# A 27-stage transformer kernel: an opening in another order, a mean summed on VectorE, two norms apart, two norms by token columns, and products of ones

## The chip, the core and the metric

The kernel runs on one NeuronCore of a Trainium2 chip. The metric is the device time of one execution in microseconds (us); less is better. Three runs of the kernel before gave 1297.25, 1302.40 and 1303.61 us, median 1302.4.

## The reference

Two blocks run over one sequence of 256 tokens with width D = 1024, all in float32. Only the parts that the change touches are shown in detail.

```python
def first_block(x, mem, ...):
    for i in range(2):
        if i == 0:
            h = rms_norm(x, norm_mix[0])
            u = h @ w_pw1 + b_pw1; a, gate = split(u, 2)            # 1024 -> 2048
            u = causal depthwise conv, 31 taps, of a * sigmoid(gate)
            x = x + silu(layer_norm(u)) @ w_pw2 + b_pw2
        else:
            x = x + diff_attention(rms_norm(x, norm_mix[1]), k, v of rms_norm(x, kv_norm), ...)
        x = x + memory_cross_attention(rms_norm(x, norm_mem[i]), mem, ...)   # 256 memory tokens
        x = x + swiglu(rms_norm(x, norm_ffn[i]), ...)                        # hidden 2816
    return rms_norm(x, norm_final)

def second_block(x, ...):
    h = x                                              # what norm_final gave
    w = rms_norm(h, attn_pre_norm) @ w_in              # then three-branch and sliding-window attention
    mixed = concat(rms_norm(o_nsa), rms_norm(o_swa)) @ w_out
    h = h + rms_norm(mixed, attn_post_norm)
    u = causal_dwconv(rms_norm(h, ffn_pre_norm) @ w_up, conv_w, conv_b)   # 3 taps, width 5632
    gate, up = split(u, 2)
    y = (gelu(gate) * up) @ w_down
    return h + rms_norm(y, ffn_post_norm)
```

## The kernel before

Activations lie turned: 128 partitions hold features, the 256 tokens run along the free dimension, and a matrix of 1024 features is 8 chunks, handled in 4 pairs of 512 columns. Weights come in tiles of 1 MB (1024 rows by 256 columns), in the order of `PLAN`. To keep float32 accuracy each tile and each activation is split: ScalarE copies it to a rounded high part (`whi`, two halves, L865 and L868), VectorE subtracts to the low part (`wlo`, L1224 and L1231), and TensorE makes three products for each pair of blocks (L470 to L472), 48 matmuls of 256 columns for a tile. Memory keys and values (`memk`, `memv`) are multiplied whole in float32 (L504).

**Order.** The order on every engine is written out by hand; semaphores tie them. There are two buffers (`raw`, `whi`, `wlo`, `acc`, each 0 and 1). The helper `ahead` stands for tile t + 2: ScalarE's copy may begin when TensorE is done with tile t, VectorE's subtraction follows it in VectorE's own order, and SP issues the next load (L389, L394) once VectorE is done with the raw data. Each engine works strictly in its order.

**Norms.** ScalarE squares (L917, L1066, L1147, L1192), GpSimd adds the four pairs into one where the name is in `SUMMED` (L435), TensorE multiplies with a matrix of ones, which sums over the features into `st` (L605), and VectorE takes the inverse root over 128x256 in 12 operations (L1269 to L1281). RMS norms scale results, not inputs: the matrix product does not wait for the norm, only its evacuation (`times_r`) does. For the output norms of the last attention the squares are summed into columns instead, one token to a partition (L630); the root is then taken of 128x4 values (`norm_columns`), and `spread` (L639) multiplies the column, broadcast, with the identity so that each partition holds the row of tokens.

**Opening.** SP loads the gains, x, tiles 0 and 1, constants, positions and memory (L376 to L385), then tile 2 on. VectorE: norm `mix0`, the subtraction for tile 2, and then per tile evacuations, subtractions, gates (`gated`) and portions of the 31-tap convolution (19 taps on VectorE, 12 as products on ScalarE added by GpSimd). TensorE goes from `pw1` (8 tiles) into `memk` (4) and `memv` (8). The mean of the layer norm is 8 products with ones (L763) set among the value tiles, the last of them behind the fifth. VectorE then centres (L1672), makes rotation angles (L1678 to L1692), subtracts for `pw2` tile 0, takes the norm, and scales (L1696).

**`win`.** Its inputs are normed twice, by `norm_final` and by `attn_pre_norm`; `Hhi` carries both gains and two square sums are made, of SQ and of SQF. GpSimd adds both in turns, and TensorE multiplies both with ones behind tile 0, ahead of tile 1.

**The end.** After the last attention: `spread("out2")`, four pairs scaled and split, `wout` (4 tiles), norm `post2`, X += normed, pairs split again, `up2` (22 tiles in 11 turns, with a 3-tap convolution on VectorE and ScalarE), `down2` (12 tiles), norm `fpost2`, X += normed, and four stores of pairs.

## Time and profile before

| what | before |
|---|---|
| median of 3 runs | 1302.4 us |
| the profiled execution | 1303.29 us |
| its span, first to last instruction | 1301.5 us |
| TensorE busy | 1197.5 us, 92% |
| VectorE busy | 909.4 us, 70% |
| ScalarE busy | 604.8 us, 46% |
| GpSimd busy | 107.9 us, 8% |
| mean granted TensorE clock | 0.958 |
| weights and inputs read | 193.08 MB |

Line numbers (L470) are those of the kernel before. PE is TensorE, PEld its weight loads, DVE VectorE, ACT ScalarE, POOL GpSimd, SP SyncE. An instruction of the timeline is: start, duration, engine, line, operation, output<-input, shape, count, and in brackets the idle time before it and what ended that. Times are us from the start of the span. A float32 matmul shows as two records, so `x4` on L605 is two products.

### The profile page before, as it was taken

The page shows a single profiled execution, that of the slowest core. Times are in us where ns is not written, and L with a number is a line of the kernel's source. Part 1 is how long each engine was busy: PE and PEld are TensorE (multiplying, and loading weights), DVE is VectorE, ACT ScalarE, POOL GpSimd, SP SyncE. Part 2 cuts the span into 40 slices and gives each one's busy share as a digit, 9 for nine tenths or more (in the row PEclk, how much of TensorE's full clock was granted, in tenths as well). Part 3 has the DMA queues.
Part 4 walks back from the last instruction along what each step waited for, and adds up shares of the span by engine and source line. Part 5 has one row for each costly group of instructions (what it writes and reads, how often), then busy time and mean ns, then how long its engine had stood idle before and what let it go on. Part 6 is the DMA issues. An engine that isn't in the chain of part 4 may idle for free.

```text
span 1301.5 us, 24008 instructions
## 1 busy us (share of the span) xinstructions
PE 1197.5 (92%) x9108; PEld 1135.3 (87%) x9108; DVE 909.4 (70%) x1503; ACT 604.8 (46%) x1027; POOL 107.9 (8%) x83
## 2 busy tenths in 40 slices
PE   5999999999999999989999999998978796899995
PEld 5988898999999999679899999998955586899995
DVE  7897776766655785656767666557886358899855
ACT  5653644544444442534453444553265343656541
POOL 1575110100000000001010000110000001000000
PEclk9999999999999999989999999998977788899998
DMA  7454352445555554124335555544540021455551
GB/s 263 161 179 146 100 192 98 150 174 175 180 194 193 177 195 165 65 102 168 120 121 176 188 190 170 193 168 160 184 188 1 1 98 65 150 175 191 192 197 65
DMA packets 32456, 197.50 MB, mean 152 GB/s; under 512 B 3712, under 2 KB 7936, under 8 KB 9472
## 3 DMA queue, kind: packets, MB, share of 16 engines
q1 hardware_dynamic: 30752, 194.14, 42.6%
q10 hardware_dynamic: 1632, 2.36, 0.5%
...
HBM read 193.08 MB, written 1.05 MB: 149 GB/s over the span
## 4 chain that ended last, share of the span: by engine, by line
PE 73%; DVE 17%; ACT 5%; issue 3%; DMA 1%; ACTq 0%; DVEq 0%; SPq 0%
PE acc L470 19%; PE acc L472 19%; PE acc L471 19%; PE acc L504 5%; DVE wlo L1231 3%; DVE wlo L1224 3%; PE acc L486 2%; ACT whi L865 2%; PE acc L739 2%; PE sc L703 1%; DVE nw L1280 1%; DVE nw L1279 1%; DMA raw<-weights 1%; PE tp L470 1%; PE tp L472 1%
## 5 line engine op out<-in xcount | busy, mean ns | idle before, releaser
L470 PE MATMUL acc<-Hhi,whi 128*128 128x256 f32 x1376 | 394.9, 287 | 17.4 <-DVE wlo L1231 17.3
L471 PE MATMUL acc<-Hlo,whi 128*128 128x256 f32 x1376 | 392.5, 285 | 0.0
L472 PE MATMUL acc<-Hhi,wlo 128*128 128x256 f32 x1376 | 392.3, 285 | 0.0
L865 ACT ACTIVATE whi<-raw 128x1024 fp32r<-128x1024 f32 x163 | 172.1, 1056 | 334.9 <-PE acc L472 310.4
L1224 DVE TENSOR_TENSOR wlo<-raw,whi 128x1024 fp32r<-128x1024 f32 x164 | 205.2, 1251 | 127.8 <-ACT whi L865 125.8
L470 PEld LDWEIGHTS acc<-Hhi,whi 128*128 128x128 f32 x1376 | 267.5, 194 | 20.6 <-DVE wlo L1231 15.0
L471 PEld LDWEIGHTS acc<-Hlo,whi 128*128 128x128 f32 x1376 | 267.5, 194 | 0.1
L472 PEld LDWEIGHTS acc<-Hhi,wlo 128*128 128x128 f32 x1376 | 267.3, 194 | 0.0
L470 PE MATMUL acc<-FH,whi 128*128 128x256 f32 x848 | 242.6, 286 | 15.7 <-DVE wlo L1231 9.3
L472 PE MATMUL acc<-FH,wlo 128*128 128x256 f32 x848 | 240.8, 284 | 0.0
L1231 DVE TENSOR_TENSOR wlo<-raw,whi 128x1024 fp32r<-128x1024 f32 x164 | 204.2, 1245 | 1.3
L470 PEld LDWEIGHTS acc<-FH,whi 128*128 128x128 f32 x848 | 163.4, 193 | 18.4 <-DVE wlo L1231 10.8
L868 ACT ACTIVATE whi<-raw 128x1024 fp32r<-128x1024 f32 x163 | 170.2, 1044 | 0.0
L472 PEld LDWEIGHTS acc<-FH,wlo 128*128 128x128 f32 x848 | 163.5, 193 | 0.0
L471 PE MATMUL acc<-FL,whi 128*128 128x256 f32 x528 | 148.1, 281 | 0.0
L435 POOL TENSOR_TENSOR SQ<-SQ 128x512 f32<-128x512 f32 x27 | 39.3, 1456 | 941.5 <-ACT SQ L917 703.9
L471 PEld LDWEIGHTS acc<-FL,whi 128*128 128x128 f32 x528 | 100.0, 189 | 0.0
L471 PE MATMUL acc<-FH,whi 128*128 128x256 f32 x320 | 92.8, 290 | 0.0
L471 PEld LDWEIGHTS acc<-FH,whi 128*128 128x128 f32 x320 | 63.8, 199 | 0.0
L470 PE MATMUL tp<-Hhi,whi 128*128 128x256 f32 x128 | 38.2, 299 | 25.2 <-DVE wlo L1224 11.9
L883 ACT ACTIVATE Hhi<-X,cst (+1 forms) x64 | 28.8, 498 | 60.9 <-DVE X L1331 37.1
L1608 DVE SCALAR_TENSOR_TENSOR sc<-A,cst,sc 128x256 f32<-128x256 f32 x136 | 54.3, 483 | 0.0
...
## 6 DMA issues: line engine op xcount, KB each, us to landing
...
```

Source lines behind the costliest of these rows:

```text
L435: ins = pool.tensor_tensor(out=q[:, 0:2, :], in0=q[:, 0:2, :], in1=q[:, 2 * p:2 * p + 2, :], op=ALU.add)
L470: pe.matmul(dst, w, x, start=first, stop=False)
L471: pe.matmul(dst, w, xl, start=False, stop=False)
L472: return pe.matmul(dst, wl, x, start=False, stop=last)
L486: mm = pe.matmul(acc[1][:, m, :], raw[k % 2][:, c, m * P:(m + 1) * P], MEM[:, c, :], start=c == 0, stop=c == KC - 1)
L504: mm = pe.matmul(acc[j][:, m, :], x[:, o] if turned else w[:, o], w if turned else x, start=c == 0, stop=c == KC - 1)
L865: act.activation(whi[j][:, 0:HALF, :], raw[j][:, 0:HALF, :], ACT.Copy).then_inc(hi_out, 1)
L868: act.activation(whi[j][:, HALF:KC, :], raw[j][:, HALF:KC, :], ACT.Copy).then_inc(hi_out, 1)
L883: ins = act.activation(dst[:, c, :], src[:, c, :], ACT.Copy, scale=gain(g0 + c))
L1224: ins = dve.tensor_tensor(out=wlo[j][:, 0:HALF, :], in0=raw[j][:, 0:HALF, :], in1=f(whi[j][:, 0:HALF, :]), op=ALU.subtract)
L1231: dve.tensor_tensor(out=wlo[j][:, HALF:KC, :], in0=raw[j][:, HALF:KC, :], in1=f(whi[j][:, HALF:KC, :]), op=ALU.subtract).then_inc(lo_dve, 1)
L1608: ins = dve.scalar_tensor_tensor(out=tap_sums[k], in0=src, scalar=w, in1=tap_sums[k], op0=ALU.mult, op1=ALU.add)
```

## The change

Ten edits:
- SP loads memory behind tiles 2 and 3 and not ahead of them.
- TensorE begins with 32 products of ones with ones, whose result nobody reads; 5 more stand ahead of `spread("out2")` and 7 ahead of `wout`.
- VectorE subtracts tile 2 ahead of norm `mix0`, and the tap portions between the `pw1` tiles are of 4 or 5 taps and not of 6 or 7.
- VectorE sums the 8 convolved chunks as it goes; TensorE makes one product with ones of the sum, behind the sixth value tile.
- ScalarE copies both `pw2` tiles ahead of the rotation's sines; VectorE subtracts them ahead of the centring and between the last pairs of the layer norm.
- `final` and `pre2` are summed one after the other by GpSimd; TensorE's product for `pre2` stands behind tile 1 of `win`.
- `fpre2` is no longer summed by GpSimd; TensorE multiplies all 8 chunks with ones.
- Norms `post2` and `fpost2` go by token columns: VectorE joins pairs 0 to 2 of the squares into one, TensorE sums into 2 columns, and the row comes by `spread` into a bank of `sc`, from which VectorE reads it.
- The subtraction of `up2` tile 1, which stood at the end of `wout`, stands behind the pairs of `post`.
- In the first turn of `up2` both evacuations and the subtraction of tile 3 stand ahead of both convolutions; ScalarE loads the Gelu table ahead of the stage.

Left out of the diff are declarations, the index list `IN_COLUMNS` that replaces `RT[...]` in the waits of `spread`, the argument `done` of `behind_split` (where its loop starts), the calls `behind(k)` after each tile of `stage` and each group of `down`, and the split of `wout`'s loop in `residual` into two turns.

```diff
-RT = {"sub": 0, "out2": 1, "attn1": 2, "pre2": 3}
+RT = {"sub": 0, "out2": 1, "attn1": 2, "pre2": 3, "post2": 1, "fpost2": 0}
 SQ_OF = {"mix0": "mix0", "ln_var": "ln", "mem0": "pw2", "ffn0": "memo0", "attn1": "down0", "mem1": "diffo", "ffn1": "memo1",
-         "pre2": "down1", "fpre2": "post"}
-SUMMED = ["mix0", "ln_var", "mem0", "ffn0", "attn1", "mem1", "ffn1", "pre2", "fpre2"]
+         "final": "down1", "pre2": "down1", "fpre2": "post"}
+SUMMED = ["mix0", "ln_var", "mem0", "ffn0", "attn1", "mem1", "ffn1", "final", "pre2"]
...
-    sp.dma_start(MEM[:, :, :], cols(mem_in)).then_inc(mem_loaded, 16)
                 load(i, j)
     late = T0["memk1"]
-    behind_split(0, WHOLE0)
+    for j in range(2):
+        sp.wait_ge(lo_dve, 1 + j)
+        load(1, j)
+    sp.dma_start(MEM[:, :, :], cols(mem_in)).then_inc(mem_loaded, 16)
+    behind_split(0, WHOLE0, 2)
...
-        sources = [SQ, SQF] if name == "pre2" else [SQ]
+        q = SQF if name == "pre2" else SQ
         for p in range(1, 4):
             pool.wait_ge(s_sq, sq.at(SQ_OF[name], p + 1))
-            for q in sources:
-                ins = pool.tensor_tensor(out=q[:, 0:2, :], in0=q[:, 0:2, :], in1=q[:, 2 * p:2 * p + 2, :], op=ALU.add)
-                if p < 3 or q is not sources[-1]:
-                    pc.link(ins)
+            ins = pool.tensor_tensor(out=q[:, 0:2, :], in0=q[:, 0:2, :], in1=q[:, 2 * p:2 * p + 2, :], op=ALU.add)
+            if p < 3:
+                pc.link(ins)
         ins.then_inc(squares_summed, 1)
...
                     mm = columns(0, xhi, xlo, m, to=to)
             mm.then_inc(tile_done, 1)
+            def stats(of, src=SQ):
+                if of in SUMMED:
+                    pe.wait_ge(squares_summed, SUMMED.index(of) + 1)
+                else:
+                    pe.wait_ge(s_sq, sq.at(SQ_OF[of]))
+                norm_stats(of, src, chunks=2 if of in SUMMED else DC)
             if norm_name:
-                if norm_name in SUMMED:
-                    pe.wait_ge(squares_summed, SUMMED.index(norm_name) + 1)
-                else:
-                    pe.wait_ge(s_sq, sq.at(SQ_OF[norm_name]))
-                chunks = 2 if norm_name in SUMMED else DC
-                if norm_name == "pre2":
-                    norm_stats("final", chunks=chunks)
-                norm_stats(norm_name, SQF if norm_name == "pre2" else SQ, chunks=chunks)
+                stats("final" if norm_name == "pre2" else norm_name)
             tile_in(L0[name] + 1)
             pe.wait_ge(acc_free, G0[name] + 2)
             columns(1, xhi, xlo, 0)
             columns(1, xhi, xlo, 1).then_inc(tile_done, 1)
+            if norm_name == "pre2":
+                stats("pre2", SQF)
+            if behind:
...
+            behind(2)
     def norm_stats(name, src=SQ, ready=None, chunks=DC):
...
-    def norm(name, before):
-        norm_stats(name, SQ, lambda k: pe.wait_ge(s_sq, sq.at(before, k // 2 + 1)) if k % 2 == 0 else None)
+    def token_sums(name, before):
+        def pair_of(p):
+            for tt in range(NT):
+                for c in (2 * p, 2 * p + 1):
+                    mm = pe.matmul(st[:, tt:tt + 1], SQ[:, c, tt * P:(tt + 1) * P], ones[:, 0:1],
+                                   start=c == tt == 0, stop=c == DC - 1 and tt == NT - 1)
+            return mm
+        def behind(k):
+            if k == 2:
+                pe.wait_ge(st_used, N0[name])
+                pe.wait_ge(squares_joined, 2 if name == "post2" else 4)
+                pair_of(0)
+                pe.wait_ge(s_sq, sq.at(before, 4))
+                pair_of(3).then_inc(stat_ready, 1)
+        return behind
     def to_tokens(name):
...
+    def meanwhile(n):
+        for _ in range(n):
+            pe.matmul(sc[:, 3, 0:P], ones[:, :], ones[:, :], start=True, stop=True)
+    pe.wait_ge(ones_ready, 1)
+    meanwhile(32)
     stage("pw1", Hhi, Hlo, source="x0", norm_name="mix0")
     pe.wait_ge(mem_loaded, 16)
     with loop(pe, 2) as i:
...
     def value_tile(k):
         whole(k % 2, "memv", 0, 8, k, turned=True, src=held[k % 2] if k >= 6 else None)
-    def mean_of(chunks):
-        for k in chunks:
-            pe.wait_ge(conv_done, 1 + k + 1)
-            mm = pe.matmul(st[:, 0:S], ones[:, :], UC[:, k, :], start=k == 0, stop=k == DC - 1)
-        return mm
-    for k in (0, 1, 2):
+    for k in range(6):
         value_tile(k)
     pe.wait_ge(st_used, N0["ln_mu"])
-    mean_of(range(5))
-    value_tile(3)
-    mean_of((5, 6))
-    value_tile(4)
-    mean_of((7,)).then_inc(stat_ready, 1)
-    value_tile(5)
+    pe.wait_ge(chunks_summed, 1)
+    pe.matmul(st[:, 0:S], ones[:, :], chunk_sum, start=True, stop=True).then_inc(stat_ready, 1)
+    value_tile(6)
     pe.wait_ge(squares_summed, SUMMED.index("ln_var") + 1)
     norm_stats("ln_var", chunks=2)
-    for k in (6, 7):
-        value_tile(k)
+    value_tile(7)
     stage("pw2", Ohi, Olo, source="ln")
     pe.wait_ge(consts_ready, 1)
     for layer, before in ((0, "pw2"), (1, "diffo")):
...
     pe.wait_ge(acc_free, G0["attn_nsa"] + 2)
     attention("attn_nsa", {3: turn_hidden, 5: compressed, 8: lambda: pe.wait_ge(cmp_ready, 1)})
+    meanwhile(5)
     spread("out2", [(2 * b + tt, sc[:, 0, b * S + tt * P:][:, 0:P]) for b in range(2) for tt in range(NT)])
-    stage("wout", Ohi, Olo, source="outn")
-    norm("post2", "wout")
+    row_of_tokens = [(tt, sc[:, 0, tt * P:(tt + 1) * P]) for tt in range(NT)]
+    meanwhile(7)
+    stage("wout", Ohi, Olo, source="outn", behind=token_sums("post2", "wout"))
+    spread("post2", row_of_tokens)
     stage("up2", Hhi, Hlo, source="post", norm_name="fpre2")
-    down("down2", "up2")
-    norm("fpost2", "down2")
+    down("down2", "up2", behind=token_sums("fpost2", "down2"))
...
                 if conv and not start:
-                    tap(i, 0, TG)()
+                    ahead(name, 0, 2, 1)
+                    tap(0, 0, TG)()
+                    tap(0, 1, TU)()
                 if start:
                     hidden(i + (-1))
                 if conv:
...
                 else:
                     acc_out(name, 2 * i)
                     act.activation(SG[:, :, :], TG[:, :, 2:2 + S], func).then_inc(s_taken, 1)
-                ahead(name, i, 2, 1, between=tap(i, 1, TU) if conv else None)
+                if start or not conv:
+                    ahead(name, i, 2, 1, between=tap(i, 1, TU) if conv else None)
         hidden(10)
     def attention(name, steps={}):
...
     value_tile(4)
+    pw2 = 16 * (T0["pw2"] // 2 + 1)
+    split(pw2, 0)
+    value_tile(5)
     for p in range(4):
         act.wait_ge(s_given, given.at("ln_sq", p + 1))
         act.activation(pair(SQ, 2 * p), pair(UC, 2 * p), ACT.Square).then_inc(s_sq, 1)
-    pw2 = 16 * (T0["pw2"] // 2 + 1)
-    split(pw2, 0)
-    value_tile(5)
+    split(pw2, 1)
+    value_tile(6)
     act.wait_ge(s_given, given.at("rope"))
     act.activation(rope_s[:, :], TG[:, 0, 0:S], ACT.Sin)
     act.activation(rope_c[:, :], TG[:, 1, 0:S], ACT.Sin).then_inc(s_taken, 1)
...
             ac.link(act.activation(SQ[:, c, :], UC[:, c, :], ACT.Silu, scale=C("ln_g", c, 1), bias=C("ln_b", c, 1)))
         act.activation(Ohi[:, 2 * p:2 * p + 2, :], SQ[:, 2 * p:2 * p + 2, :], ACT.Copy).then_inc(s_taken, 1)
         if p == 1:
-            value_tile(6)
-    split(pw2, 1)
-    value_tile(7)
+            value_tile(7)
     residual("pw2", 2, [(Hhi, "g_mem0")])
     for layer in range(2):
...
     ready_chunks("post", X, Hhi, "g_fpre2")
+    act.activation(ske[:, 0, 0:1], gsub[:, 0:1], ACT.Gelu_apprx_tanh)
     ffn("up2", ACT.Gelu_apprx_tanh)
     residual("down2", 6, [], last_stage=True)
...
                     weights(ks[:-1])
+                    if name in ("wout", "down2") and start:
+                        dve.wait_ge(s_sq, sq.at(name, 2 + g))
+                        dve.wait_ge(squares_joined, g + (0 if name == "wout" else 2))
+                        dve.tensor_tensor(out=SQ[:, 0:2, :], in0=SQ[:, 0:2, :], in1=SQ[:, 2 + 2 * g:4 + 2 * g, :], op=ALU.add)\
+                            .then_inc(squares_joined, 1)
                     tile(name, i, per, ks[-1])
...
-                evacuate(name, i, 0, times_r(TG[:, :, 2:2 + S], 0, not start), norm_name, gate_conv, between=True)
+                if not start:
+                    tile(name, 0, 2, 0)
+                    ahead(name, 0, 2, 0)
+                    norm(norm_name)
+                    out_acc(times_r(TG[:, :, 2:2 + S], 0, True)())
+                    tile(name, 0, 2, 1)
+                    out_acc(times_r(TU[:, :, 2:2 + S], 1)())
+                    ahead(name, 0, 2, 1)
+                    gate_conv()
+                    up_conv()
+                else:
+                    evacuate(name, i, 0, times_r(TG[:, :, 2:2 + S], 0), norm_name, gate_conv, between=True)
                 if start:
                     dve.wait_ge(s_given, 2 * i + given.at(name, 0))
                     hidden_rest(name, i + (-1), up)
                     dve.wait_ge(s_h, i + h.at(name, 0))
-                evacuate(name, i, 1, times_r(TU[:, :, 2:2 + S], 1), norm_name, up_conv, between=True)
+                    evacuate(name, i, 1, times_r(TU[:, :, 2:2 + S], 1), norm_name, up_conv, between=True)
                 dve.wait_ge(s_taken, 2 * i + taken.at(name, 1))
                 for k in range(2):
...
+    ahead("pw1", 0, 8, 0)
     norm("mix0")
-    ahead("pw1", 0, 8, 0)
     pw1_tile(0)
     pw1_tile(1)
     ahead("pw1", 0, 8, 1)
     gated(0)
     pw1_tile(2)
     ahead("pw1", 0, 8, 2)
-    conv_taps(0, 0, 6)
+    conv_taps(0, 0, 5)
     pw1_tile(3)
     ahead("pw1", 0, 8, 3)
     gated(1)
-    conv_taps(0, 6, 12)
+    conv_taps(0, 5, 9)
     pw1_tile(4)
     ahead("pw1", 0, 8, 4)
-    conv_taps(0, 12, DVE_TAPS)
-    conv_end(0)
+    conv_taps(0, 9, 13)
     pw1_tile(5)
     ahead("pw1", 0, 8, 5)
     gated(2)
-    conv_taps(1, 0, 6)
+    conv_taps(0, 13, 17)
     pw1_tile(6)
-    conv_taps(1, 6, 12)
+    conv_taps(0, 17, DVE_TAPS)
+    conv_end(0)
+    conv_taps(1, 0, 5)
     pw1_tile(7)
-    conv_taps(1, 12, DVE_TAPS)
+    conv_taps(1, 5, 10)
     gated(3)
+    conv_taps(1, 10, DVE_TAPS)
     conv_end(1)
-    for c in range(2, DC):
-        conv_taps(c, 0, DVE_TAPS)
-        conv_end(c)
+    for c in range(2, DC + 1):
+        ins = dve.tensor_tensor(out=chunk_sum, in0=UC[:, 0, :] if c == 2 else chunk_sum, in1=UC[:, c - 1, :], op=ALU.add)
+        if c < DC:
+            ch.link(ins)
+            conv_taps(c, 0, DVE_TAPS)
+            conv_end(c)
+    ins.then_inc(chunks_summed, 1)
+    ahead("memv", 0, 8, 6)
     dve.wait_ge(stat_ready, N0["ln_mu"] + 1)
     for p in range(4):
...
     link(dve.tensor_scalar(r0, r0, -PI_IN, PI_IN, op0=ALU.max, op1=ALU.min))
     link(dve.scalar_tensor_tensor(out=r1, in0=r0, scalar=-1.0, in1=r0, op0=ALU.mult, op1=ALU.max))
     dve.tensor_scalar(r1, r1, -1.0, math.pi / 2, op0=ALU.mult, op1=ALU.add).then_inc(s_given, 1)
-    ahead("memv", 0, 8, 6)
     norm("ln_var", eps=LN_EPS)
     for p in range(4):
         dve.tensor_tensor(out=pair(UC, 2 * p), in0=pair(UC, 2 * p), in1=both(R[:, :]), op=ALU.mult).then_inc(s_given, 1)
-    for p in range(4):
+    def ln_rest(p):
         dve.wait_ge(s_taken, taken.at("ln", p + 1))
         dve.tensor_tensor(out=Olo[:, 2 * p:2 * p + 2, :], in0=SQ[:, 2 * p:2 * p + 2, :],
                           in1=f(Ohi[:, 2 * p:2 * p + 2, :]), op=ALU.subtract).then_inc(s_h, 1)
-    ahead("memv", 0, 8, 7)
+    ln_rest(0)
+    ahead("memv", 0, 8, 7, between=lambda: ln_rest(1))
+    ln_rest(2)
+    ln_rest(3)
...
+    def row_ready(name):
+        norm_columns(name, NT, D, RMS_EPS)
+        dve.wait_ge(spread_ready, IN_COLUMNS.index(name) + 1)
     def add_normed(done):
         def add(p):
-            link(dve.tensor_tensor(out=pair(MG, 2 * p), in0=pair(MG, 2 * p), in1=both(R[:, :]), op=ALU.mult))
+            link(dve.tensor_tensor(out=pair(MG, 2 * p), in0=both(sc[:, 0, 0:S]), in1=pair(MG, 2 * p), op=ALU.mult))
             dve.tensor_tensor(out=pair(X, 2 * p), in0=pair(X, 2 * p), in1=pair(MG, 2 * p), op=ALU.add).then_inc(done, 1)
         return add
+    row_ready("post2")
     by_pairs("post", add_normed(s_given), Hlo, X, Hhi, "g_fpre2")
+    ahead("wout", 1, 2, 1)
     dve.memset(TG[:, :, 0:2], 0.0)
     link(dve.memset(TU[:, :, 0:2], 0.0))
     conv_ffn("up2", "fpre2")
     residual("down2", 6, [], last_stage=True)
-    norm("fpost2")
+    row_ready("fpost2")
     for p in range(4):
         add_normed(x_final)(p)
```

## Rows read from the trace of the kernel before

**Rows 1.** The page, busy time by engine and the chain of waits by engine
```profile
PE 1197.5 (92%) x9108; PEld 1135.3 (87%) x9108; DVE 909.4 (70%) x1503; ACT 604.8 (46%) x1027; POOL 107.9 (8%) x83
...
PE 73%; DVE 17%; ACT 5%; issue 3%; DMA 1%; ACTq 0%; DVEq 0%; SPq 0%
```

**Rows 2.** Windows: stretch, length, busy PE PEld DVE ACT POOL, granted clock, DMA
```profile
11.90:15.20 3.30, 3.25 (x15) 3.25 (x16) 1.47 (x2) 3.30 (x6) 2.10 (x2) 1.00 1.00 376
...
28.00:32.40 4.40, 4.39 (x24) 4.39 (x25) 4.22 (x6) 2.35 (x4) 0.00 (x0) 0.62 0.69 238
1134.00:1157.00 23.00, 23.00 (x194) 23.00 (x193) 21.30 (x35) 14.28 (x22) 0.00 (x0) 1.00 0.54 182
962.00:1037.00 75.00, 62.71 (x468) 41.40 (x468) 43.50 (x135) 38.25 (x142) 0.00 (x0) 0.74 0.08 29
...
1044.00:1049.60 5.60, 5.46 (x25) 5.49 (x26) 3.65 (x8) 1.82 (x4) 0.00 (x0) 0.50 0.00 0
```

**Rows 3.** Timeline of the opening
```profile
11.95 0.58 PE L470 MATMUL tp<-Hhi,whi 128*128 128x256 f32 x1 [11.95 <-DVE wlo L1224]
...
28.01 0.39 PE L470 MATMUL acc<-Hhi,whi 128*128 128x256 f32 x1 [1.95 <-DVE wlo L1231]
...
23.18 1.06 ACT L865 ACTIVATE whi<-raw 128x1024 fp32r<-128x1024 f32 x1 [2.80 <-DMA raw<-weights]
...
20.35 0.42 DVE L1269 TENSOR_SCALAR nw<-st 128x256 f32<-128x256 f32 x1 [0.27 <-PE st L605]
```

**Rows 4.** Chain of waits (first row) and timeline, memory tiles to `pw2`
```profile
67.04 48.35 PE acc L504 x224
...
132.77 2.48 DVE L1672 SCALAR_TENSOR_TENSOR A<-st,A 128x512 f32<-128x512 f32 x4 [9.23 <-PE st L763]
...
141.99 1.22 DVE L1224 TENSOR_TENSOR wlo<-raw,whi 128x1024 fp32r<-128x1024 f32 x1
...
161.38 0.39 PE L470 MATMUL acc<-FH,whi 128*128 128x256 f32 x1 [0.90 <-DVE wlo L1231]
```

**Rows 5.** Timeline of the first tiles of `win`
```profile
876.08 1.13 PE L605 MATMUL st<-SQ,ones 128*128 128x256 f32 x4 [1.25 <-POOL MKV L435]
879.76 0.80 PE L605 MATMUL st<-MKV,ones 128*128 128x256 f32 x1 [2.56 <-DVE nw L1269]
...
911.66 0.58 PE L470 MATMUL acc<-Hhi,whi 128*128 128x256 f32 x1 [5.02 <-DVE wlo L1231]
...
891.05 1.23 DVE L1224 TENSOR_TENSOR wlo<-raw,whi 128x1024 fp32r<-128x1024 f32 x1 [6.55 <-ACT whi L865]
...
873.89 2.13 POOL L435 TENSOR_TENSOR MKV<-MKV 128x512 f32<-128x512 f32 x1
```

**Rows 6.** Timeline of TensorE: `spread` for `sub`, for `out2`, first pair of `wout`
```profile
572.42 3.84 PE L639 MATMUL sc<-cst,rt 128*128 128x128 f32 x32 [0.69 <-ACT MKV L953]
...
1039.33 2.08 PE L639 MATMUL sc<-cst,rt 128*128 128x128 f32 x8 [2.43 <-DVE rt L1281]
...
1044.14 0.55 PE L470 MATMUL acc<-FH,whi 128*128 128x256 f32 x1 [2.73 <-DVE FH L1259]
```

**Rows 7.** Timeline from the end of norm `post2` to tile 3 of `up2`
```profile
1079.94 0.69 DVE L1855 TENSOR_TENSOR MKV<-MKV,R 128x512 f32<-128x512 f32 x1
...
1086.55 1.77 DVE L1855 TENSOR_TENSOR MKV<-MKV,R 128x512 f32<-128x512 f32 x1
...
1093.12 1.06 ACT L865 ACTIVATE whi<-raw 128x1024 fp32r<-128x1024 f32 x1 [2.61 <-PE tp L472]
...
1111.22 0.58 PE L470 MATMUL acc<-Hhi,whi 128*128 128x256 f32 x1 [5.82 <-DVE wlo L1231]
```

**Rows 8.** Timeline of the end
```profile
1284.62 3.62 PE L605 MATMUL st<-SQ,ones 128*128 128x256 f32 x16
...
1293.52 0.69 DVE L1855 TENSOR_TENSOR MKV<-MKV,R 128x512 f32<-128x512 f32 x1
```

34 lines of the change are left out of this document (22 added, 12 removed).

## The prediction

> **What bounds the kernel now.** I read the page first. TensorE is busy for 92% of the span and holds 73% of the chain that ended last [rows 1], and in the long feed-forward stages it never stops: 194 matmuls in 23.0 us, 0.119 us each, at the full clock [rows 2]. So nothing is to be won there; the change must earn its time where TensorE waits. The timelines of the places that the diff touches show those waits: 11.95 us before the first tile and 1.95 before the third [rows 3], 0.90 at 161.38 [rows 4], 1.25, 2.56 and 5.02 in `win` [rows 5], 2.43 and 2.73 after the last attention [rows 6], 5.82 in the first turn of `up2` [rows 7], and all that follows the last matmul [rows 8]. After most of them the granted clock is at its lower level (1.2 GHz) for a while, so a wait costs more than its length [rows 2].
>
> All sums are against the profiled execution: 1303.3 us, of which the span is 1301.5. The median of the runs is 1302.4, 0.9 less.
>
> **A, opening and layer norm.** Ones: 32 products of 128x128. The same shape took 3.84/16 = 0.24 us at the full clock and 2.08/4 = 0.52 at half [rows 6]; so 7.7 to 16.7 us from about 1.1 on. Tile 0 itself ran its first 3.3 us at about 0.22 us a matmul [rows 2], then at 0.12. With the same delay the ones take some 9.5 us and end before 11.95, and tile 0 gains the 15 slow matmuls x 0.1 = 1.5 us. That alone buys little, because tile 1 waits for its low half (18.98); it starts 0.9 us sooner.
> Load: memory (1 MB) moves behind two weight loads on SP's queue. ScalarE waited 2.80 us for the third tile's data until 23.18 [rows 3]; now the data should be there at about 19.5 and the copy starts once ScalarE has done the exponential at 20.4. Memory is read only at 67, some 35 us after it lands; nothing queued behind it is due sooner.
> The subtraction of tile 2 now precedes the norm, which began at 20.35 [rows 3]: it ends at 23.9, the norm at 29.1 and not 25.6. TensorE runs tile 2 from 24.8 (before 28.01), then waits about 2.2 us for tile 3's low half at 32.7. Such a wait was followed at 28.0 by 24 matmuls in 4.39 us instead of 2.9: 1.5 us lost [rows 2]. I count that loss in half. The smaller tap portions then bring tiles 6 and 7 (waits 1.6 and 0.65) nearer. `pw1` ends 3 to 5 us sooner, at 62 to 64.
> From there 48.35 us for 7 tiles of memory products [rows 4], 6.9 us each, set the pace. Before, the last mean product stood after 9 tiles and started VectorE at 132.77; now it stands after 10, at 131 to 133.2 plus 0.5. The seven additions on VectorE (7 x 0.46 = 3.2 us) lie in its 9.2 us of idling before 132.77 [rows 4]. But the subtraction for `pw2` tile 0 (2.3 us) now stands ahead of the centring and waits for a load that is issued after value tile 4: it ends at 132.6 to 134.8, and that starts the centring: -0.2 to +2.0. In exchange it is gone from between rope and norm, where it ran at 141.99 [rows 4]: -2.3. So the norm is 0.2 to 2.4 sooner. `pw2`'s second tile no longer waits for its split (0.90 [rows 4]), worth 0.1 to 1.1; TensorE, though, has no tile left between value tile 7 and the first pair, about 4 us, and may restart at half clock (0 to -1.5). I take **-2.0**, bounds +1.5 and -3.9.
>
> **B, two norms of `win` summed apart.** GpSimd finishes the `final` sum first, so TensorE's 1.25 us wait goes. Tile 1 no longer stands behind the second sum's products, which waited 2.56 us for VectorE to read the first sum: it starts with its low half at 877.1, not at 881.8, and ends at 883, not 889.3. VectorE idled 6.55 us until 891.05 for that tile's end [rows 5]; then it is busy without a break to 912 and decides TensorE's 5.02 us wait at 911.66. So the gain is VectorE's: up to 6.5. Against it, GpSimd now adds three pairs of the second square sum after 873.8 where one stood (2.13 us [rows 5]). VectorE's 128x512 multiply took 0.69 alone and 1.77 beside such an addition [rows 7]: 1.1 us per extra addition, two of them, 0 to 2.2; I take 1.9. **-4.6**, bounds -6.5 and -1.6 (tile 1 at half clock).
> The Trainium skill ("SBUF — State Buffer", Who interferes with whom) says the two engines' common port is an exclusive lock for a whole instruction. By that rule VectorE also waits for the third addition, 3 x 1.3 = 3.9 in all, less 1.1 paid before: -3.7 in place of -4.6. The rows fit a delay of that size (1.77 - 0.69 = 1.08).
>
> **C, ones around `out2`.** Five ones (1.2 to 2.6 us) lie in TensorE's wait of 2.43, seven (1.7 to 3.6) in the one of 2.73 [rows 6]. At worst they hold the pair back by 0.2 + 0.9. What they buy is the clock: from 1044.0 to 1049.6 it was 0.50, 25 matmuls in 5.5 us [rows 2], and the four spread products 2.08 instead of 0.96. I assume `wout` starts at the full clock and the spread does not: tile 0 then ends 1.5 us after its fourth pair (1047.9), 3.1 sooner. **-3.1**, bounds -4.3 and +1.1.
>
> **D1, `post2` by token columns.** Eight 256-column products (3.6 us for the same at the end [rows 8]) become eight one-column ones, four of them behind the last square. The 12 wide norm operations (5.25 us) become narrow ones (2.35, the wait in rows 6 is theirs), plus two spread products (0.5 to 1.0). The subtraction of `up2` tile 1 (2.3 us), which stood ahead of the norm, goes behind the pairs. From the end of `wout` (1069.8) to VectorE's first multiply: 10.1 us before (1079.94 [rows 7]), now 0.9 copy + 0.8 square + 0.8 products + 2.4 + 0.6 = 5.6: -4.5. The two joins of squares on VectorE (0.7 each) lie in its waits for tiles. The squares of `fpre2` leave GpSimd, so the pairs lose no time to it (two operations of 1.1 extra [rows 7]): -2.0. TensorE takes the pairs at half clock longer than before: +0.3. **-6.2**, bounds -7.0 and -4.5.
>
> **D2, first turn of `up2`.** TensorE sums eight chunks (3.5 us, not 0.9) before tile 1. VectorE's norm does not feel it: it waited for the subtraction of tile 2 anyway, 3.5 us after the end of tile 0 (1093.1, [rows 7]). TensorE then runs tiles 1 and 2 until 15.0 us after tile 0. Tile 3's subtraction now comes right behind tile 1's evacuation, ahead of both convolutions, and is ready at 12.7. Tile 3 starts at 15.0 instead of 18.1 (1111.22 - 1093.1): -3.1; the half-clock stretch after the 5.82 us wait goes too, -1.3; VectorE is behind by its convolutions and costs one wait of 0.7. The Gelu table's load (1.3 us on ScalarE) is off this path. **-3.7**, bounds -4.6 and -2.0.
>
> **E, the end.** Before: 3.6 us of products from 1284.62, norm, first multiply at 1293.52 [rows 8]. Now 1.6 to the last square, 0.8, 2.4, 0.6: 1290.1. **-3.4**, bounds -3.8 and -2.8.
>
> Sum: -2.0 - 4.6 - 3.1 - 6.2 - 3.7 - 3.4 = -23.0. 1303.3 - 23.0 = 1280.3, and 0.9 less on the scale of the median: **1279.4**. The bounds together give 1272 to 1293.
>
> **The rivals.**
> 1. The ones do not keep the clock. They run at 0.52 each: tile 0 starts at 17.8, which the later waits absorb to about 2 us; C becomes +1.1, and the pairs of D1 and E's spread cost 1.5 more. -23 + 2 + 4.2 + 1.5 = -15.3: 1287. For it: at 1022 to 1037 the clock went up and down beside work of this kind (mean 0.74 in that attention [rows 2]). Against: they fill both waits almost wholly.
> 2. The three additions each stop VectorE for good and tile 3 of `win` comes late (B at -1.6): 1282. The lock named under B lies between this and the forecast.
> 3. Everything lands at its good bound (clock up throughout): 1274.
> 4. Slower. The last attention, 75 us with TensorE busy for 62.7 at a mean clock of 0.74 [rows 2], starts some 7 us earlier relative to the clock's ups and downs. If it fell to 0.50 throughout, its 62.7 us became 62.7 x 0.74/0.50 = 92.8: +30, 1309. It decides from +23 on, a mean clock below 0.54. Against: the same products reach the full clock again and again, and part of them is not on the path.
>
> **Chances.** Forecast 0.62 (its own range 1275 to 1285), rival 1 0.16, rival 2 0.08, rival 3 0.12, rival 4 0.02. The range 1272 to 1290 takes in all but the outer half of rival 1 and rival 4. A measurement can tell about 0.5%, 6.5 us, from no change; all but rival 4 and a sliver of rival 1 lie beyond that: faster 0.95, within 0.03, slower 0.02.
>
> **What would show it.** A: TensorE's first tile at the full rate; norm of `ln_var` before 144; a gap ahead of `pw2`. B: no TensorE gap over 1.5 us between 875 and 884, VectorE's idle 6.55 us under 1. C: clock 1.00 in the first tile of `wout`. D: 5.6 us from `wout` to the first multiply; no wait over 1 us before `up2` tile 3. E: 5.5 us from last matmul to first multiply. Wrong if `up2` or `down2`, 173 us together, lengthen, if the ones push a stage back, or if the last attention moves by more than 3 us.

## The result, and the profile after

| what | before | after |
|---|---|---|
| median of 4 runs each, on one chip | 1300.04 us (1297.25 to 1303.61) | 1278.36 us (1275.39 to 1279.67) |
| the profiled execution, its span | 1303.29, 1301.5 us | 1277.8, 1276.0 us |
| TensorE, VectorE, GpSimd busy | 1197.5, 909.4, 107.9 us | 1198.0, 910.2, 104.1 us |
| mean granted clock | 0.958 | 0.967 |

The ratio is 0.983, 95% interval 0.980 to 0.986: 21.7 us less; the two profiled spans differ by 25.5. The forecast was 1279.4 us (-23.0), range 1272 to 1290. It was worked out from a median of 1302.4; a fourth run of the kernel before made that 1300.04, so -23.0 is to be compared with -21.7. TensorE's busy time is as large as before although some 14 us of it are now ones; what went is waiting, norm products and matmuls at half clock. A matmul of a weight tile starts 0.12 us after the one before it at the full clock and 0.21 at half; the text calls the latter slow.

The page after, busy time and the chain of waits by engine, against [rows 1]:

```profile
PE 1198.0 (94%) x9202; PEld 1137.2 (89%) x9202; DVE 910.2 (71%) x1514; ACT 605.4 (47%) x1028; POOL 104.1 (8%) x80
...
PE 74%; DVE 16%; ACT 4%; issue 3%; DMA 1%; DVEq 0%; ACTq 0%; SPq 0%
```

TensorE's timeline after, the places of [rows 3 to 8] at which it still waits, in order: the ones, tile 0, the fourth tile of `pw1` (tiles 1 and 2 run without a break before it), `pw2` and its fourth tile, the last tile of `down1` (in no row), `win` tile 1, `win` tile 5, `wout`, the column products and the spread of `post2`'s norm, `up2`, its tile 4, and the same products and spread at the end. Here and below a line number is that of the kernel whose trace is shown.

```profile
1.07 8.94 PE L787 MATMUL sc<-ones 128*128 128x128 f32 x64 [1.07 <-DVE ones L1622]
...
12.25 0.39 PE L476 MATMUL tp<-Hhi,whi 128*128 128x256 f32 x1 [2.25 <-DVE wlo L1261]
...
32.86 0.39 PE L476 MATMUL acc<-Hhi,whi 128*128 128x256 f32 x1 [1.68 <-DVE wlo L1268]
...
150.27 0.35 PE L476 MATMUL acc<-FH,whi 128*128 128x256 f32 x1 [3.86 <-DVE FH L1758]
...
170.26 0.39 PE L476 MATMUL acc<-FH,whi 128*128 128x256 f32 x1 [1.02 <-DVE wlo L1268]
...
835.99 0.39 PE L476 MATMUL acc<-FH,whi 128*128 128x256 f32 x1 [1.31 <-DVE wlo L1268]
...
869.82 0.39 PE L476 MATMUL acc<-Hhi,whi 128*128 128x256 f32 x1 [1.50 <-DVE wlo L1268]
...
900.00 0.58 PE L476 MATMUL acc<-Hhi,whi 128*128 128x256 f32 x1 [5.18 <-DVE wlo L1268]
...
1033.15 0.35 PE L476 MATMUL acc<-FH,whi 128*128 128x256 f32 x1 [0.49 <-DVE FH L1296]
...
1057.97 1.05 PE L630 MATMUL st<-ones,SQ 128*128 128x1 f32 x8 [0.76 <-ACT SQ L950]
...
1061.44 1.23 PE L671 MATMUL sc<-cst,rt 128*128 128x128 f32 x4 [2.42 <-DVE rt L1318]
...
1066.38 0.55 PE L476 MATMUL tp<-Hhi,whi 128*128 128x256 f32 x1 [3.72 <-DVE Hlo L1296]
...
1095.29 0.38 PE L476 MATMUL acc<-Hhi,whi 128*128 128x256 f32 x1 [0.91 <-DVE wlo L1268]
...
1263.11 1.25 PE L630 MATMUL st<-ones,SQ 128*128 128x1 f32 x8 [0.66 <-ACT SQ L950]
...
1266.77 1.22 PE L671 MATMUL sc<-cst,rt 128*128 128x128 f32 x4 [2.42 <-DVE rt L1318]
```

Each bracket is the wait; compare 1.95 before the third tile, 5.82 in `up2`'s first turn and 2.73 before `wout` [rows 3, 6, 7]. The wait of 5.18 before `win`'s tile 5 is left. Windows after (length, busy PE PEld DVE ACT POOL, granted clock): tile 0, tiles 1 and 2, the first 5.3 us of `wout`.

```profile
12.10:18.30 6.20, 6.01 (x48) 5.81 (x48) 4.32 (x4) 4.12 (x7) 4.75 (x3) 1.00 0.90 339
18.30:31.20 12.90, 12.86 (x100) 12.25 (x100) 11.17 (x25) 6.01 (x8) 0.00 (x0) 1.00 0.68 246
...
1033.10:1038.40 5.30, 5.25 (x44) 5.28 (x45) 3.56 (x8) 1.82 (x4) 0.00 (x0) 1.00 0.00 0
```

Tile 0's 48 matmuls take 6.0 us (before 7.5), and `wout` starts with 44 in 5.3 us where it had 25 in 5.6 [rows 2]. VectorE and GpSimd after, around the norm of `final`:

```profile
867.48 2.29 DVE L1268 TENSOR_TENSOR wlo<-raw,whi 128x1024 fp32r<-128x1024 f32 x1
...
869.68 2.30 DVE L1261 TENSOR_TENSOR wlo<-raw,whi 128x1024 fp32r<-128x1024 f32 x1
...
871.91 2.31 DVE L1268 TENSOR_TENSOR wlo<-raw,whi 128x1024 fp32r<-128x1024 f32 x1
...
874.14 0.41 DVE L1306 TENSOR_SCALAR nw<-st 128x256 f32<-128x256 f32 x1
...
879.38 1.22 DVE L1261 TENSOR_TENSOR wlo<-raw,whi 128x1024 fp32r<-128x1024 f32 x1
```

```profile
866.43 6.71 POOL L441 TENSOR_TENSOR MKV<-MKV 128x512 f32<-128x512 f32 x3
```

VectorE goes from the norm into the subtraction at 879.38 with no idle time (6.55 before [rows 5]); the three subtractions ahead of the norm took 2.3 us each beside GpSimd's three additions. VectorE around the layer norm of the opening: subtraction for `pw2`, centring, norm (the last began at 144.26 before):

```profile
130.05 1.23 DVE L1261 TENSOR_TENSOR wlo<-raw,whi 128x1024 fp32r<-128x1024 f32 x1 [2.87 <-ACT whi L898]
...
132.33 2.48 DVE L1732 SCALAR_TENSOR_TENSOR A<-st,A 128x512 f32<-128x512 f32 x4
...
141.53 0.42 DVE L1306 TENSOR_SCALAR nw<-st 128x256 f32<-128x256 f32 x1
```

The difference of the two traces, accumulated at common instructions:

| stretch | predicted | measured |
|---|---|---|
| A: opening, through `pw2` | -2.0 | -4.4 |
| end of `down1` (in no step) | 0 | -3.0 |
| B: `win` | -4.6 | -4.3 |
| last attention | 0 | +0.6 |
| C: `wout` | -3.1 | -2.4 |
| D1: `post2`, tile 0 of `up2` | -6.2 | -6.0 |
| D2: first turn of `up2` | -3.7 | -3.7 |
| E: the end | -3.4 | -2.4 |
| sum | -23.0 | -25.6 |

The rows round to 0.1 beside the span's 25.5.

### The profile page after: what moved, and what is told of

Its sections match the earlier page's. It is cut to its first block, busy times and chain, and to the rows that moved or that the text cites. A ratio compares the mean times of both kernels' runs of the same rounds, so it can differ in the third digit from the quotient of the medians.

```text
span 1276.0 us, 24166 instructions
## 1 busy us (share of the span) xinstructions
PE 1198.0 (94%) x9202; PEld 1137.2 (89%) x9202; DVE 910.2 (71%) x1514; ACT 605.4 (47%) x1028; POOL 104.1 (8%) x80
## 4 chain that ended last, share of the span: by engine, by line
PE 74%; DVE 16%; ACT 4%; issue 3%; DMA 1%; DVEq 0%; ACTq 0%; SPq 0%
PE acc L476 19%; PE acc L478 19%; PE acc L477 19%; PE acc L510 5%; DVE wlo L1268 3%; DVE wlo L1261 2%; PE acc L492 2%; PE acc L771 2%; ACT whi L898 2%; DMA raw<-weights 1%; PE sc L735 1%; DVE nw L1317 1%; DVE nw L1316 1%; PE tp L476 1%; PE tp L760 1%
## 5 line engine op out<-in xcount | busy, mean ns | idle before, releaser
L441 POOL TENSOR_TENSOR SQ<-SQ 128x512 f32<-128x512 f32 x24 | 34.8, 1451 | 729.4 <-ACT SQ L950 700.6
L1296 DVE SCALAR_TENSOR_TENSOR Hlo<-X,cst,Hhi (+1 forms) x64 | 36.6, 615 | 21.2 <-ACT Hhi L916 16.3
```

Of the source, the lines that this page charges most:

```text
L441: ins = pool.tensor_tensor(out=q[:, 0:2, :], in0=q[:, 0:2, :], in1=q[:, 2 * p:2 * p + 2, :], op=ALU.add)
L1296: ins = dve.scalar_tensor_tensor(out=dst[:, k, :], in0=src[:, k, :], scalar=col(name, c + k), in1=f(hi[:, k, :]), op0=ALU.mult, op1=ALU.su ...
```

## The experiments

Each was timed 5 to 7 times beside the kernel before. The executions of one kernel scatter by 3 to 11 us and the interval of a ratio is 5 to 8 us wide, so that, but for `sums_apart_alone`, the intervals overlap or touch. An edit of 1 to 3 us is read from one trace of it: the starts of VectorE's 328 subtractions of weight tiles and of TensorE's matmuls, instruction by instruction, against the changed kernel's. Where a kernel differs only behind a point, the stretch ahead of it shows how large a difference chance makes.

| kernel | median us | ratio to before (95%) | span of the profiled execution, us |
|---|---|---|---|
| no_ones_open | 1277.90 | 0.982 (0.979 to 0.984) | 1276.8 |
| no_ones_out | 1278.63 | 0.983 (0.980 to 0.986) | 1279.0 |
| in_turns | 1275.91 | 0.982 (0.979 to 0.984) | 1272.2 |
| more_ones | 1275.58 | 0.981 (0.979 to 0.984) | 1270.9 |
| sums_apart_alone | 1293.76 | 0.995 (0.992 to 0.997) | 1292.3 |
| mem_early | 1280.22 | 0.984 (0.981 to 0.986) | 1277.6 |
| up2_old_turn | 1281.04 | 0.985 (0.982 to 0.988) | 1276.1 |
| fpre2_gpsimd | 1281.80 | 0.986 (0.983 to 0.988) | 1276.5 |
| old_fpost2 | 1280.62 | 0.985 (0.983 to 0.987) | 1279.9 |
| mean_products | 1280.52 | 0.986 (0.984 to 0.989) | 1275.0 |
| norm_first | 1280.65 | 0.985 (0.983 to 0.987) | 1280.0 |
| turns_and_ones | 1277.35 | 0.983 (0.981 to 0.985) | 1276.1 |

**The opening, four runs.**

```
 mem_early:      load(MEM) back ahead of tiles 2 and 3 on SP's queue
 norm_first:    -ahead("pw1", 0, 8, 0)
                 norm("mix0")
                +ahead("pw1", 0, 8, 0)
 mean_products:  mean_of(...) on TensorE as before; the chunk_sum additions go
 no_ones_open:  -meanwhile(32)
```

> The changed kernel with the memory load back ahead of the third and fourth weight tile on SP's queue. Theory: the data of tile 2 land some 2.5 us later (copy at 23.2 and not at 20.65), the norm of mix0 stands behind that subtraction and ends 2.5 us later, and so do tile 0's evacuation and tile 3: pw1 ends 2 to 3 us later and the memory products and the layer norm with it: +2 to +3. Rival: VectorE's convolution portions and the following tiles absorb it, as later waits did with other delays: 0 to +0.8.

> The changed kernel with VectorE's norm of mix0 ahead of the subtraction of the third tile, as before; the memory load stays behind the two weight loads. Theory: the norm ends at 25.7, the third tile's low half at 28.1 and not 24.1, TensorE waits 2.8 us for it and may take the tile behind at half clock; the fourth tile's is there in time: pw1 +1.2 to +2.7 us. Rival: the evacuation of tile 0 comes 1 us sooner and the rest of pw1 hangs on that: -1 to 0.

VectorE in mem_early:

```profile
25.32 1.23 DVE L1258 TENSOR_TENSOR wlo<-raw,whi 128x1024 fp32r<-128x1024 f32 x1 [4.83 <-ACT whi L895]
...
27.60 0.42 DVE L1303 TENSOR_SCALAR nw<-st 128x256 f32<-128x256 f32 x1
...
32.84 0.69 DVE L1676 TENSOR_TENSOR TG<-tp,R 128x512 f32<-128x512 f32 x1
```

TensorE in norm_first:

```profile
27.18 0.58 PE L476 MATMUL acc<-Hhi,whi 128*128 128x256 f32 x1 [2.61 <-DVE wlo L1268]
```

With the early memory load the third tile's subtraction waits 4.83 us for its copy and starts at 25.32, not 21.72; the norm and all that follows are 3.6 later. At `pw2` it is +3.9, above what I expected. In norm_first the norm is done at 24.8, but TensorE waits 2.61 for the low half of the third tile and then starts slowly (0.58 for the first matmul). At `pw2` it stands 2.5 later though this run had begun 0.8 sooner: 3.3. In both, 14 or 15 matmuls of the third tile are slow. The predicted step (memory's load behind two weight loads, the subtraction ahead of the norm) holds; its parts can't be had singly.

> The changed kernel with the layer norm's mean formed by eight products among the memory products again, and no additions on VectorE. Theory: TensorE gives seven products of 256 columns more (0.47 us each, 3.3 us) where its memory products set the pace: the fifth value tile and with it the low half for pw2, which stands ahead of the centring, come 2.5 to 3.3 us later, and so does pw2: +2.5 to +3.3. Rival: VectorE, rid of 3.2 us of additions, sets the pace: -1 to 0.

```profile
132.85 1.23 DVE L1271 TENSOR_TENSOR wlo<-raw,whi 128x1024 fp32r<-128x1024 f32 x1 [9.31 <-ACT whi L908]
...
135.13 2.48 DVE L1738 SCALAR_TENSOR_TENSOR A<-st,A 128x512 f32<-128x512 f32 x4
```

The subtraction starts at 132.85 (130.05 in the changed kernel, in a run that began 0.45 sooner): 3.3 us, the seven products. VectorE idled 9.31 us ahead of it, so the additions are free, as predicted. Each of three edits, undone by itself, costs 3.3 to 3.9 of the 4.4 us that the opening brings as a whole: they stand in one chain, and the chain falls back to its next latest member. Seven traces with this same opening stand 3.3 to 4.6 us ahead of before behind `pw2`, so chance moves it by about 1 us. The smaller tap portions and the early copies and subtractions for `pw2` were not undone singly.

> The changed kernel without its 32 products ahead of tile 0. Theory: they are worth little, because tile 1 waits for its low half at 19.40 us whatever tile 0 does: tile 0 starts with about 15 matmuls at 0.22 us and ends 1.2 to 1.5 us later, at 19.5 to 19.8, so that the whole costs +0.1 to +0.5 us, and the gain of 4.4 us in the opening comes from the load, the subtraction and the portions. Rival: the clock is what the opening gained beyond the predicted 2.0 us, through tile 3 too: +1.5 to +2.5 us, with a stretch of half clock after the wait ahead of tile 3.

Tile 0 had 16 matmuls at 0.21 us. But this run's first tile also came 1.2 us later (13.49 against 12.25), and at the start of `pw2` it is +1.5 in all, so some 0.2 is left for the ones. (The first tile of `pw2` then has 23 slow matmuls here and 15 in the changed kernel, 0.9 us more; three traces that have the ones have 22 to 25 there too, so this is chance.) In ten of eleven traces with the ones tile 0 runs at full rate, in the three without it has 14 to 24 slow matmuls. The exception is more_ones, where 17 of its matmuls were slow with the same 32 ones ahead. The ones in the opening are worth little, 0.2 us by this one trace; the theory stands.

**The ones around `out2`.**

```
-meanwhile(5)
 spread("out2", ...)
-meanwhile(7)
```

> The changed kernel without the 5 and the 7 products around out2's spread. Theory: the first tile of wout runs at half clock again, 25 matmuls in 5.5 us as before: wout ends +2.4 us later relative to the end of the attention, and the time rises by 2.4 (2.0 to 2.9). Rival: the stage had the full clock without them, because it stands elsewhere in time than before: 0.

Windows of no_ones_out:

```profile
1034.10:1039.40 5.30, 5.27 (x26) 5.30 (x27) 3.54 (x8) 1.81 (x4) 0.00 (x0) 0.54 0.01 3
```

26 matmuls in 5.3 us, not 44. From the norm of `out2` to `wout`'s first matmul the kernels with and without the ones take 7.2 us (7.06 to 7.25 in all fourteen), and `wout` takes 25.1 us to its last matmul, not 23.0: the clock alone is the gain, 2.1 us. The rival (0) falls. Eleven traces of kernels with these ones have no slow stretch in `wout`; the three without (before, sums_apart_alone, no_ones_out) have 24, 18 and 21 slow matmuls. The five and the seven ones were not taken out separately.

**`final` and `pre2`, two runs.**

```
 in_turns: for p in range(1, 4):
+              add pair p of SQ; add pair p of SQF     # as before
 sums_apart_alone: the kernel before, with only the two sums apart
                   and pre2's products behind tile 1
```

> The changed kernel with GpSimd's two sums taken in turns, pair by pair, as before; the norms' order on TensorE stays. Theory: the addition for SQF at pair 2 meets VectorE's subtraction ahead of the last tile of down1 again: that costs 1.1 us there, TensorE waits 2.4 instead of 1.3 us and falls to half clock, +3.0 in all by 867; in win two of three colliding additions go, which gives back 1.0 to 2.2. Sum +0.8 to +2.0, and win alone is faster. Rival (the prediction's own step, in which down1 plays no part): -2.2 to 0, with tile 0 of win where the changed kernel has it.

> The kernel before with part B alone: GpSimd sums the squares of final and of pre2 one after the other, TensorE sends pre2's products behind tile 1. Theory: the collision of 1.1 us at the end of down1 goes; whether the half clock behind that wait (about 1.9 us of the 3.0) goes too is open, because with the same wait of 2.38 us it was absent in another run; win itself gives 4.3. So -5.4 without and -7.3 with the clock, and the three additions in a row slow three subtractions of VectorE to 2.3 us. Rival (the prediction's step): down1 stays, win gives 4.6: -4.6.

VectorE at the end of `down1` and in `win` in in_turns, and the wait of sums_apart_alone:

```profile
834.16 2.29 DVE L1284 TENSOR_TENSOR wlo<-raw,whi 128x1024 fp32r<-128x1024 f32 x1
...
868.42 2.29 DVE L1284 TENSOR_TENSOR wlo<-raw,whi 128x1024 fp32r<-128x1024 f32 x1
...
870.63 1.21 DVE L1277 TENSOR_TENSOR wlo<-raw,whi 128x1024 fp32r<-128x1024 f32 x1
...
872.90 0.41 DVE L1322 TENSOR_SCALAR nw<-st 128x256 f32<-128x256 f32 x1
```

```profile
840.86 0.39 PE L469 MATMUL acc<-FH,whi 128*128 128x256 f32 x1 [1.31 <-DVE wlo L1229]
```

By itself the edit takes 1.1 us up to the wait in the last tile of `down1`, 3.0 up to `win` (the clock behind the wait), and 7.3 up to `win`'s tile 5; the timed medians say 6.7. The rival (-4.6) falls, and the -3.0 that stand in no step of the prediction are this edit's. Taking the sums in turns again gives the other half of the picture: +1.1 at `down1` (a subtraction of 2.29, a wait of 2.39), and in `win` only one subtraction of 2.29 in place of three: -1.9 up to tile 5. By the end of `win` the trace shows -2.6, but the 0.7 between is mostly clock: behind tile 5's wait in_turns has 15 slow matmuls and the changed kernel 24, and traces whose `win` is the changed kernel's have 16 or 17, or 22 to 24. So TensorE's order is what `win` gains by (that is the difference left; the order was not undone alone); the additions in a row cost 1.9 there and save 1.1 at `down1`, with or without the clock. That dip is no certain thing: behind a wait of 2.4 us TensorE fell to half clock for 14 and 15 matmuls in before and turns_and_ones and not at all in in_turns; behind one of 1.3 in none of eleven.

**`post2`, `fpost2` and `up2`, three runs.**

```
 fpre2_gpsimd: SUMMED = [..., "final", "pre2", "fpre2"]
 up2_old_turn: evacuate(tile 0, with its convolution); evacuate(tile 1, with its)
 old_fpost2:   eight 256-column products and norm("fpost2") over 128x256
```

> The changed kernel with the squares of fpre2 summed by GpSimd again (2 chunks for TensorE, not 8). Theory: two of the additions fall beside VectorE's multiplies, adds and rests of the pairs and cost it 1.1 us each, which shifts tile 0 of up2, bound by those pairs, by 2.0 to 2.2; the 2.7 us less of products ahead of tile 1 are swallowed by the wait for the norm's evacuation: +2.0. Rival: the shorter sums bring tiles 1 to 3 forward as well: -0.7 to +0.5.

GpSimd and VectorE in it:

```profile
1066.49 1.72 POOL L441 TENSOR_TENSOR SQ<-SQ 128x512 f32<-128x512 f32 x1 [193.59 <-ACT SQ L1228]
1068.67 1.36 POOL L441 TENSOR_TENSOR SQ<-SQ 128x512 f32<-128x512 f32 x1 [0.46 <-ACT SQ L1228]
```

```profile
1066.99 1.90 DVE L1296 SCALAR_TENSOR_TENSOR Hlo<-X,cst,Hhi 128x256 fp32r<-128x256 f32 x2
...
1068.82 0.68 DVE L1922 TENSOR_TENSOR MKV<-sc,MKV 128x512 f32<-128x512 f32 x1
1069.53 1.05 DVE L1923 TENSOR_TENSOR X<-X,MKV 128x512 f32<-128x512 f32 x1
...
1072.36 2.32 DVE L1261 TENSOR_TENSOR wlo<-raw,whi 128x1024 fp32r<-128x1024 f32 x1
```

The first addition costs the rest of a pair 1.0 us (1.90, not 0.88), the second 0.36, the third a subtraction 1.1 that has time. The second is the one that the theory priced too high: it meets the multiply `MKV<-sc,MKV`, which reads the row from `sc`, a PSUM tensor, and runs at its usual 0.68 us beside the addition; only the next operation is held, by 0.36. In the kernel before, the same addition met `MKV<-MKV,R`, with both inputs in SBUF, and made 1.77 of 0.69 [rows 7]. So the kernel's other edit, the row in `sc`, had already removed part of this price. +1.4 by the last pair. The rival's part is there too: with the shorter sums tile 3 stands 0.5 us ahead of the changed kernel's, but tile 4 then waits 2.45 us, not 0.91, and +1.2 is left at the end: between theory (+2.0) and rival.

> The changed kernel with the first turn of up2 in its old order on VectorE and ScalarE (each tile's convolution ahead of the next evacuation and subtraction); the squares of fpre2 are still summed by TensorE. Theory: tile 3 of up2 waits 3 us for its low half, and TensorE takes the tile behind at half clock for 1.3 us, while the wait of 0.9 ahead of tile 4 goes: +2.5 to +3.7. Rival: the order of the turn gives nothing and the gain came with the freed GpSimd: 0 to +0.5.

```profile
1087.72 0.58 PE L476 MATMUL acc<-Hhi,whi 128*128 128x256 f32 x1 [3.25 <-DVE wlo L1265]
```

The wait for the fourth tile is back, 3.25 us; from tile 0 to tile 4 the stretch is 4.8 us longer, more than predicted (3.7) and expected. Some 1.1 of that is chance: 25 matmuls are slow behind the wait here, 13 in before, and 26 in sums_apart_alone, whose code is that of before in this stage.

> The changed kernel with the last norm (fpost2) as before: eight 256-column products, twelve wide operations, no join of the squares on VectorE. Theory: from the last matmul to VectorE's first multiply 8.7 us as before and not 6.4: +2.4, all behind the last matmul, which stays where it is. Rival (the prediction's step): +3.4.

```profile
1271.94 0.69 DVE L1923 TENSOR_TENSOR MKV<-R,MKV 128x512 f32<-128x512 f32 x1
```

TensorE's sums begin at 1263.03, so the norm takes 8.9 us to the first multiply; in the changed kernel 6.5 (1261.50 to 1268.03): +2.4, the theory. The same edit for `post2` was not undone by itself.

**More ones, and a version put together.**

```
+meanwhile(14) ahead of pw2;  +meanwhile(16) ahead of win's tile 5
+meanwhile(8) ahead of spread("post2"), +meanwhile(14) behind it
+meanwhile(8) ahead of spread("fpost2")
```

> The changed kernel with more unread products of ones: 14 ahead of pw2 (wait 3.86 us), 16 ahead of tile 5 of win (wait 5.19), 8 ahead of the spread of post2 and 14 behind it (waits 2.42 and 3.72), 8 ahead of the spread of fpost2 (2.42). Theory: each stretch behind them keeps the full clock: pw2 -1.3 (14 matmuls at 0.21 instead of 0.12), win -1.8, spread and tile 0 of up2 -0.6 and -1.3, the last spread -0.6: -5.6 us in all. Rival A: the ones themselves fall to 0.52 us each as the five ahead of out2 did, and end after the data: pw2 +3.4, win +3.1, post2 +1.8 and +3.6, fpost2 +1.8, up to +13.7. Rival B: the clock falls or stays with no regard to them: 0.

TensorE in more_ones, and its window from tile 5 of `win` on (first), beside the changed kernel's (second):

```profile
1055.28 2.03 PE L791 MATMUL sc<-ones 128*128 128x128 f32 x16
...
1057.84 0.71 PE L675 MATMUL sc<-cst,rt 128*128 128x128 f32 x4 [0.53 <-DVE rt L1326]
```

```profile
897.50:905.00 7.50, 5.90 (x51) 5.71 (x51) 7.36 (x10) 1.72 (x2) 0.00 (x0) 1.00 0.38 120
```

```profile
900.00:907.50 7.50, 7.50 (x43) 7.50 (x44) 6.11 (x8) 0.00 (x0) 0.00 (x0) 0.64 0.65 226
```

Behind each of the added ones TensorE ran at the full clock: 0.71 us for the spread (1.23 in the changed kernel). In `win` they gave 2.4 us against the changed kernel's trace with its 24 slow matmuls, 1.6 to 1.8 against traces with 16 or 17; at the spreads 0.5 and 0.7. At `pw2` they gave nothing (19.0 us to the third tile's end with and without, though 15 matmuls are slow without): the pairs of VectorE set that pace. Against four traces in which 22 to 25 matmuls were slow there it is 0.7 to 1.1 us. In `up2` the next tile came about 1 us sooner than in eight other traces, where 20 to 26 matmuls behind the wait were slow, but no sooner than in the changed kernel's own trace, with 12.

> A version put together: the changed kernel with GpSimd's sums in turns, 16 more products of ones ahead of tile 5 of win, 8 ahead of the spread of post2 and 8 ahead of that of fpost2. Theory: the parts add up as their runs had them: turns -2.6 in win and +1.1 at down1, ones in win -2.4, spreads -0.5 and -0.6: -5.0. Rival: with the sums in turns VectorE reaches tile 5 sooner and the wait is too short for 16 products, which hold TensorE up: -1 to -2.5.

It is not shown to beat the changed kernel: 1277.35 us, interval of the ratio 0.981 to 0.985 against 0.980 to 0.986. In `win` it gains 4.3 of the 5.0 us expected, but this run had the collision and the half clock at `down1` (+2.6) and 26 slow matmuls in `up2`, and the last ones ran partly at half clock (3.06 us for 8) and gave 0.1 for 0.7.

**What chance does.** The last attention is the same code in all fourteen traces. Windows over it, changed kernel and in_turns:

```profile
951.00:1025.90 74.90, 60.80 (x469) 40.27 (x469) 42.88 (x134) 38.26 (x142) 0.00 (x0) 0.77 0.09 29
```

```profile
949.00:1021.00 72.00, 56.13 (x469) 37.73 (x469) 43.13 (x134) 38.32 (x142) 0.00 (x0) 0.82 0.09 30
```

The same 469 matmuls take 60.8 us at a mean clock of 0.77 and 56.1 at 0.82. Over the fourteen traces the attention lasts 71.7 (clock 0.81) to 77.7 us (0.74). `diffo`, unchanged too, has 25 matmuls at half clock in some traces and none in others (2.6 us). Scatter of this size is enough to hide an edit of 3 us in five or six executions.

## Why the prediction was right, point by point

The sum was right within 2.6 us of the span, in part by luck: A and the end of `down1` brought 5.4 us more than forecast, B, C, D1 and E 2.2 less, and the last attention took 0.6 more by chance. Two sums of the prediction are off by a little without consequence: the terms of D1 make 5.5 us and not 5.6, and the worst bounds together give 1294, not 1293.

- **Method.** The forecast looked for TensorE's waits. The gain came from them, from the norm products on the path, and from the half clock behind the waits: before has 156 slow weight matmuls in stretches outside the last attention and after 80, at 0.09 us more each 7 of the 25.5 us.
- **A**, predicted -2.0, measured -4.4. `pw1` ended at 61.92, inside the 62 to 64 forecast within rounding. On the way "such a wait was followed at 28.0 by 24 matmuls in 4.39 us" did not come again: the wait before tile 3 was 1.68 and nothing was lost behind it. The step that was mis-sized is the sum behind `pw1`. The low half for `pw2` was taken to move the centring by -0.2 to +2.0; it began 0.4 sooner (132.33 for 132.77), and with the 2.3 of the moved subtraction the norm came 2.7 sooner, outside the 0.2 to 2.4. The other 1.7 came in `pw2`: before, the memory products held TensorE some 1.6 us beyond the first ready pair (it started at 154.51), now it waits for the pair (3.86). Of that I had counted little. The full rate in tile 0 bought almost nothing, as said.
- **The end of `down1`**: no step had it. The prediction priced GpSimd's additions only where they were added, not where they were taken away. In the trace of before VectorE's subtraction at the end of `down1` stood at 2.29 us beside GpSimd's addition to MKV, and I had not read it. VectorE's and GpSimd's timeline of before there:

```profile
839.09 2.29 DVE L1231 TENSOR_TENSOR wlo<-raw,whi 128x1024 fp32r<-128x1024 f32 x1
```

```profile
838.16 2.14 POOL L435 TENSOR_TENSOR MKV<-MKV 128x512 f32<-128x512 f32 x1
```

sums_apart_alone shows what it is worth: 3 us with the clock behind it.
- **B**, -4.6 and -4.3. VectorE was the cause, its 6.55 us of idling went, and TensorE has no gap over 1.5 between 869 and 888. Three subtractions stand at 2.3 us where one did: two more, at 1.1 us each, cost 2.2, and 6.5 less 2.2 is the 4.3 measured. The prediction had the same two with 1.9, and in_turns gives 1.9 back up to tile 5. By the rule of the Trainium skill ("SBUF — State Buffer", Who interferes with whom), an exclusive lock under which VectorE waits for GpSimd's whole instruction, the forecast was -3.7. The trace agrees with that rule nearly: each of the three subtractions lost 1.1 us (2.29 to 2.31, alone 1.22), a little less than the 1.3 us that an addition takes by itself. With 1.1 in place of 1.3 that sum gives the 2.2.
- **C**, -3.1 and -2.4 (2.1 by its experiment). The mechanism held: spread at half clock, `wout` at the full one. The mis-sized term is "tile 0 ends 1.5 us after its fourth pair": 48 matmuls take 5.8 us from the first pair at full clock, so tile 0 is TensorE's, and only the slow matmuls come back (24 before, at 0.09 us).
- **D1**, -6.2 and -6.0. From `wout` to the first multiply 6.3 us, forecast 5.6: the spread ran at half clock (1.23, not 0.6). That is 3.8 less than before, not 4.5. From the first multiply to the last rest of a pair it took 11.0 us before and 8.8 after: the freed GpSimd gave the predicted 2.0 and a little more, although putting it back in the changed kernel costs only 1.4, because there the row is in `sc`. The 0.3 for pairs at a lower clock did not come.
- **D2**, -3.7 and -3.7: one wait of 0.91 (forecast 0.7), none before tile 3. Undone it costs 4.8, and the half-clock stretch behind the old wait is 13 or 26 matmuls long by chance, so the agreement to the tenth is luck.
- **E**, -3.4 and -2.4: 6.4 us, not 5.5, from the last matmul to the first multiply. The spread took 1.22 and not 0.6, and the second group of one-column products 1.25, not 0.8: both terms had been taken at the full clock.
- **The rivals.** Rival 1 (ones do not keep the clock) is half seen: the five ahead of the spread ran at 0.50 us each and the spread too, but the seven behind it sufficed. Rival 2 (B at -1.6) did not come: its collisions are there, at the 1.9 to 2.2 us that the forecast held. Rival 3 did not come. Rival 4 (last attention slower) did not come: there is a scatter of 6 us between traces of the same code, far from the 23 that it needed.
